# Both state copies of mixer B issued in routing, and five gated rows instead of six made by ScalarE in each pair of groups

## What is computed

```python
s = jnp.einsum('thcd,hcnd->thcn', q, sub_keys)
v1, i1 = lax.top_k(s[:, :, 0], PEER_TOPK); v2, i2 = lax.top_k(s[:, :, 1], PEER_TOPK)
...
coef = g * jax.nn.gelu(a);  y = jnp.einsum('thk,thkd->td', coef, v_tab[expert])
...
k_ext = jnp.concatenate([state_b_k[l], kb], axis=1); v_ext = jnp.concatenate([state_b_v[l], vb], axis=1)
bks.append(k_ext[:, -n_buf:]); bvs.append(v_ext[:, -n_buf:])
```

## Time and profile before

| | us |
|---|---|
| runs of the kernel before | 3879.78, 3879.08, 3867.53 |
| their median | 3879.08 |
| the profiled execution, its own time | 3876.23 |
| its span, from the first to the last instruction | 3874.3 |
| routing, from its first DMA issue to its last | 1228.6 to 1755.0 |
| spreading, from its first DMA issue to the first of experts | 1758.0 to 2025.2 |
| experts | 2025.2 to the end |

### The profile page before, as it was taken

How to read it: one execution, slowest core, us unless ns; L and a number is a source line. 1 busy time by engine, 2 the same in 40 slices (tenths; PEclk the granted TensorE clock), 3 DMA queues, 4 the chain that set the end, 5 groups by cost and what they waited for, 6 DMA issues and landing times. The chain is left out here.

```text
span 3874.3 us, 63692 instructions
## 1 busy us (share of the span) xinstructions
PE 3248.0 (84%) x22587; PEld 2865.8 (74%) x22587; DVE 2795.4 (72%) x6612; ACT 1219.9 (31%) x2349; POOL 1210.2 (31%) x1214
## 2 busy tenths in 40 slices
PE   7997676688836877746737999999999999999998
PEld 5776344455523655535637999999999999999998
DVE  5552443322211688999837999999999999999998
ACT  4442232333401232218952222222222222222221
POOL 0001022122211000000003556565656565555554
PEclk9998788899967888878978999999999999999999
DMA  4323667777675333305999999999999999999997
GB/s 139 117 68 108 196 219 246 229 233 236 212 273 196 131 131 125 131 11 184 329 300 344 346 342 336 337 352 336 344 347 347 334 336 357 343 329 343 349 335 279
DMA packets 405619, 993.05 MB, mean 256 GB/s; under 512 B 38002, under 2 KB 165972, under 8 KB 404116
## 3 DMA queue, kind: packets, MB, share of 16 engines
q0 software_dynamic: 150048, 595.57, 43.0%
q1 hardware_dynamic: 252996, 383.53, 29.0%
q10 hardware_dynamic: 2368, 11.54, 0.8%
HBM read 911.56 MB, written 146.44 MB: 273 GB/s over the span
## 5 line engine op out<-in xcount | busy, mean ns | idle before, releaser
L2105 PE MATMUL banks<-x_hi,u_hi 128*128 128x320 f32 x2048 | 633.8, 309 | 61.5 <-DVE x_lo L2195 61.5
L2118 PE MATMUL banks<-coef_hi,v_hi 128*128 128x320 f32 x2048 | 633.6, 309 | 6.4 <-issue 6.4
L2105 PE MATMUL banks<-x_lo,u_hi 128*128 128x320 f32 x2048 | 633.6, 309 | 0.0
L2105 PE MATMUL banks<-x_hi,u_lo 128*128 128x320 f32 x2048 | 633.6, 309 | 0.0
L2118 PE MATMUL banks<-coef_lo,v_hi 128*128 128x320 f32 x2048 | 633.5, 309 | 0.0
L2118 PE MATMUL banks<-coef_hi,v_lo 128*128 128x320 f32 x2048 | 633.4, 309 | 0.0
L2066 POOL DMA_INDIRECT uv_row<-in_v_rows,expert_tok x384 | 477.7, 1244 | 386.5 <-DVE y_tok L2249 334.5
L2066 POOL DMA_INDIRECT uv_row<-in_u_rows,expert_tok x384 | 455.5, 1186 | 360.8 <-DVE dots L2223 313.4
L2249 DVE SCALAR_TENSOR_TENSOR y_tok<-uv_row,share,y_tok 128x1024 f32<-128x1024 f32 x415 | 530.3, 1278 | 1.0 <-DVE y_tok L2249 0.4
L2223 DVE CUSTOM_DVE_ANT_0 uv_row<-uv_row,x_tok 128x1024 f32<-128x1024 f32 x416 | 506.3, 1218 | 0.0
L2105 PEld LDWEIGHTS banks<-x_hi,u_hi 128*128 128x128 f32 x2048 | 385.3, 188 | 61.7 <-DVE x_lo L2195 61.7
(11 more groups left out here) (254 smaller groups left out, 5531.7 us busy)
## 6 DMA issues: line engine op xcount, KB each, us to landing
values_ps<-in_cache_v POOLq DMA_DIRECT2D x256, 256.0 KB, 3.9
keys_ps<-in_cache_k SPq DMA_DIRECT2D x256, 256.0 KB, 4.5
uv_raw<-in_u SPq DMA_DIRECT2D x128, 512.0 KB, 7.4
uv_raw<-in_v SPq DMA_DIRECT2D x128, 512.0 KB, 7.1
scratch_gates<-stage SPq DMA_DIRECT2D x10, 4096.0 KB, 29.6
gates<-scratch_gates SPq DMA_DIRECT2D x128, 320.0 KB, 6.2
out_win_k_out<-in_state_k POOLq DMA_DIRECT2D x8, 4088.0 KB, 14.8
out_win_v_out<-in_state_v POOLq DMA_DIRECT2D x8, 4088.0 KB, 17.8
```

The lines of the kernel that those rows point to most:

```text
L2105: ins = nc.tensor.matmul(bank[:, 2 * r + c, 0:CH], u[r][a][:, k * P:(k + 1) * P], x2[b][:, k, c * CH:(c + 1) * CH], start=(k == 0 and a == b),
L2118: ins = nc.tensor.matmul(bank[:, 4 + n % 4, 0:CH], v[j][a][:, k * P:(k + 1) * P], coef[j][b][:, c * CH:(c + 1) * CH], start=(j == 0 and a ...
```

## The change

In routing POOL calls `move_state` for the key state and then for the value state of the same sample, both behind the same wait for `h_ready`, so that 16 large and 16 small DMAs are issued there; its last wait counts 64 for each sample. Spreading loses its POOL block and the semaphore of the value copies. In spreading ScalarE makes three gated rows of a group with an even number and two of a group with an odd number; VectorE makes the other five or six. The buffers stay as they are.

```diff
                     pool.wait_ge(h_ready, b + 1)
                     move_state(pool, io, 0, b, state_moved)
-                pool.wait_ge(state_moved, 32 * DB)
+                    move_state(pool, io, 1, b, state_moved)
+                pool.wait_ge(state_moved, 64 * DB)
...
-        state_moved = sems("state_v_moved")
...
+        def by_act(g):
+            return BY_ACT - g % 2
...
-                for j in range(E_GROUP - BY_ACT):
+                for j in range(E_GROUP - by_act(g)):
...
-        @block.gpsimd
-        def _(pool):
-            for b in range(DB):
-                since(pool, staged, b * (GROUPS // DB))
-                move_state(pool, io, 1, b, state_moved)
-            pool.wait_ge(state_moved, 32 * DB)
...
-                toks = [slice(n, n + 1) for n in range((g + 1) * E_GROUP - BY_ACT, (g + 1) * E_GROUP)]
+                toks = [slice(n, n + 1) for n in range((g + 1) * E_GROUP - by_act(g), (g + 1) * E_GROUP)]
...
-                    ins = nc.scalar.activation(row2[g % RING][:, E_GROUP - BY_ACT + n, :], apart[:, g % 2, n, :], ACT.Relu,
+                    ins = nc.scalar.activation(row2[g % RING][:, E_GROUP - by_act(g) + n, :], apart[:, g % 2, n, :], ACT.Relu,
```

## The result

| | us |
|---|---|
| forecast | 3849.0 (3837 to 3868) |
| the changed kernel, median of 6 runs (3832.11 to 3838.90) | 3835.52 |
| the kernel before, with the runs taken beside it, median of 6 (3855.55 to 3879.78) | 3867.91 |
| ratio, with its 95% interval | 0.9914 (0.9894 to 0.9935) |
| the profiled execution of after: its own time, its span | 3832.11, 3830.6 |

Three of the six runs of before are the ones known ahead of the prediction; the three new ones took 3855.55, 3863.60 and 3868.29 us. The change makes the kernel 0.86% faster: the medians lie 32.4 us apart, and the interval of the ratio is worth 25 to 41 us.

What follows compares the result with a forecast made beforehand. Spreading was taken as bound by ScalarE with DMA close behind, routing by VectorE. Gain 27.2 us: 20.5 for rounds, 8.2 for the stage wait, 1.5 given back; 3876.23 - 27.2 = 3849.0 us, range 3837 to 3868.

Steps and rivals of the forecast that it cites:

- ScalarE sets spreading's pace, DMA lies just behind it: Spreading before the change: ScalarE limits at 234 us, with 243.8 us of full DMA engines as a second limit.
- no going in step: Spreading: the engines' alternating rounds average out, so VectorE's mean of 2.545 us a group counts, 203.6 for 80 groups.
- Rival (a): Spreading: each group goes at its slower maker's pace, 219.0 us for 80 groups, gain 11.8, time 3864.5; chance 0.08.
- (b): Spreading: only the wait on stage goes, ScalarE's round having a hidden floor; 8.2 us gained, 3868.0; chance 0.06 with (e).
- (e): Spreading: the table's stores remain the bound, at under three quarters of their rate alone; chance 0.06 with (b).
- 8.2 for the wait: Spreading: ScalarE's two waits for earlier stores to leave stage, 8.2 us in all, vanish once the value copies leave.
- The tail of 31.3 us stays: Spreading's end, from ScalarE's last copy into stage to experts' first load, stays 31.3 us; no gain counted.
- The copies are hidden in routing: Routing: key and value copies land in some 30 us of a 52.4 us tile, with 22 us of room; no time added.
- Rival (c): Routing: the pair of copies overruns its tile at 60.8 us, costing 67 us in eight tiles, time 3916; chance 0.05.
- (d): Routing: VectorE is held while POOL issues the value pair, 0.99 us in each of eight tiles, 7.9 us; chance 0.04.
- The 0.05 us read from the earlier trace: Spreading before: VectorE's five gated rows take 1.41 instead of 1.36 us beside a value copy's issue by POOL.
- The level from which the sum starts: Whole kernel: the sum starts from one profiled execution of 3876.23 us, with 12 us allowed on either side.

Runs made afterwards that it cites:

- the copies alone: Against the kernel before, only the value copies move to routing; ScalarE keeps three gated rows in every group: 3858.59 us, ratio 0.9983.
- the rows alone: Against the kernel before, only the gated rows are shared anew, three and two by turns; value copies stay in spreading: 3858.70 us, ratio 0.9987.
- the kernel with the copies twice: Changed kernel with both state copies of each tile made a second time in routing once the first pair has landed: 3835.86 us, ratio 0.9928.
- the runs with POOL's rows: Changed kernel with one or two gated rows of each spreading group made by GpSimd, two by ScalarE, the rest by VectorE: 3827.82 and 3839.52 us.
- the third profile of before: The kernel before without edit, profiled again for the stretch ahead of routing: routing begins at 1210.9 us; its single run took 3855.78 us.
- the kernel with POOL's two rows: Changed kernel with two gated rows of each spreading group made by GpSimd, four by VectorE, two by ScalarE: 3839.52 us, ratio 0.9926.

## Why the prediction was right in its steps and wrong in its time

- *ScalarE sets spreading's pace, DMA lies just behind it.* Right, and both halves were shown by leaving one in place: the copies alone leave ScalarE as the pace, the rows alone run into full DMA engines.
- *The engines' new rounds, 2.42 and 2.67 us by turns for VectorE, and no going in step.* Right: 206.9 us for the groups against 206.8. Rival (a), which would have given 219.0 for the 80 groups, is out. So are (b) and (e), which would have left spreading at 259.0 us: it takes 240.0, ScalarE's round did shrink, and the DMA engines stand for 11 us between two stores.
- *The division of the gain into 20.5 for the rows and 8.2 for the wait.* Right as a sum for both together, wrong if read as what each would bring alone: the rows alone bring 6.5. The prediction put both limits side by side and didn't say that the rows' 20.5 needs the copies out of the way.
- *The tail of 31.3 us stays.* Right, 31.3.
- *The copies are hidden in routing.* Right: routing is 526.6 to 528.9 us with them and 526.9 to 529.4 without, and even twice the copies don't change it. Rival (c) put its point at a pair that outlasts a tile; the experiment went past that, and the stores still landed in 46.6 us at most: under copies that never stop they slow down, but they don't wait for the copies' end.
- *VectorE held by POOL's issues* (d): no. VectorE is busy 47.48 us in a tile of routing with four issues as with two. In the tile shown, the value pair's issue (1397.52 to 1398.50) falls into VectorE's pause of 1.75 us, as the prediction had it, so that the changed kernel by itself tests (d) little. In the kernel with the copies twice the second issues fall beside VectorE's work (for one, its searches of L1661 at 1334 to 1337), and routing still takes 528.4. The 0.05 us read from the earlier trace rows is one case: beside five other issues of value copies in that trace VectorE's five rows take 1.36 or 1.37 us. The section "Who interferes with whom" of the page SBUF — State Buffer in the Trainium skill speaks of such a hold; no run here shows VectorE held for POOL's time, not even with POOL busy without a pause. What the runs with POOL's rows show is the other direction: POOL's row stands while VectorE makes one-hots.
- *The level from which the sum starts.* This is the step that failed. I subtracted 27.2 from one execution of 3876.23 us and gave the result 12 us to either side, because three runs lay 12 us apart. But that execution and two of the three runs (3879.08 and 3879.78) lie above all 46 later runs of before, whose highest is 3875.78: before's stretch ahead of routing was 1228.6 us there and 1210.9 and 1216.1 in the later profiles, and its median was 3864.38 over 25 runs beside the later kernels. From that level the same sum gives 3837.2; the changed kernel's medians are 3835.52 and 3831.91. So 11.9 of the 13.5 us by which the forecast was too high are the level. A spread of three runs taken together was used as if it bounded the level of all runs.

What stays open: the stretch ahead of routing varies by up to 19 us over the same code. The traces place it in the attention over the paged cache: POOL's first instruction there starts at 369.46 to 371.47 us in the ten profiles, and its last load of values (L633) is issued at 1058.31 us in the third profile of before and at 1077.33 in the kernel with POOL's two rows, 19.0 of the 19.2 us between the two. What varies in that phase was not tried, and why three of the first four executions were that long isn't known. And of the difference of whole times beside each other, 3864.38 - 3831.91 = 32.5 us with an interval of 24 to 41, spreading explains 26.7; the rest is inside the interval and was not followed.

## What to carry to other kernels

Where a phase has two limits within a few per cent of each other, here an engine's round and the DMA engines, a change that eases only one brings little (8.5 or 6.5 us), and both together bring more than the sum (26.7): look for the second limit before an edit is judged by itself. Copies that nobody waits for belong where the DMA engines are idle and another engine is the bound, and their room is how late the other transfers there may land, not how long the copies take. The difference of two stretches inside a trace was here forecast within 2% (27.2 us against 26.7 on the mean of the profiles); an absolute time is only as good as the level it starts from, which one execution and three runs don't give.

## What the runs showed of the hardware that was not expected

- GpSimd's form of the gated row takes 0.79 us (3.97 for five) while VectorE makes no one-hots, against 0.255 for a further one on VectorE and 0.59 for the two instructions on ScalarE. A row that starts beside the one-hots stands until they are made, so that it takes up to 2.2 us. VectorE is hardly slowed: beside POOL's rows four of its own take mostly 1.11 us, five mostly 1.36 (1.42 to 1.56 in four groups), and its one-hots 1.20 to 1.23.
- Stores of 4 MB in rows of 512 bytes, alone on the DMA engines, run at a share of 1.04 and 290 GB/s. Of two copies of 4088 KB from DRAM to DRAM issued 0.97 us apart, the first lands after 15.5 us and the second after 27.4, nearly twice one alone (15.2 us).
